# A second home for the last five weight units of every expert, used by odd experts

## The reference

```
combine = einsum("nk,nke->ne", top_w, one_hot(top_idx, N_EXPERTS))   # two experts a token
g = einsum("nd,edf->nef", t, w_gate)                                  # 16 experts, 1024 x 1024 each
u = einsum("nd,edf->nef", t, w_up)
a = silu(g) * u * combine[:, :, None]
y = einsum("nef,efd->nd", a, w_down)                                  # 1024 x 1024 each
x = x + g2 * y ; y_out = rms_norm(x, norm_final)
```

## Time and profile before

| | us |
|---|---|
| median of 3 runs | 836.02 (828.83 to 836.41) |
| the profiled execution, whole | 833.07 |
| its span, first to last instruction | 831.4 |
| TensorE busy / DVE / ACT / POOL | 746.8 / 311.8 / 187.1 / 43.3 |
| experts, first gate matmul to last down matmul | 326.2 to 803.8 |
| mean DMA rate over the span | 314 GB/s |

### The profile page before, as it was taken

One profiled execution on the slowest core, in us unless ns is written; L12 is line 12 of the kernel. 1 busy time (PEld: TensorE's weight loads), 2 busy tenths in 40 slices (PEclk: granted clock), 3 DMA queues, 4 the chain that ended last, 5 costly groups with the idle time before them and its releaser, 6 DMA issues.

```text
span 831.4 us, 22823 instructions
## 1 busy us (share of the span) xinstructions
PE 746.8 (90%) x9748; PEld 412.1 (50%) x9749; DVE 311.8 (38%) x802; ACT 187.1 (22%) x392; POOL 43.3 (5%) x102
## 2 busy tenths in 40 slices
PE   5699986788999988999998999999999999999862
PEld 5345553474644466553552654554544554555232
DVE  3898969997012266211210121211201211121138
ACT  3555340200022133021211122201201112221132
POOL 2000100000010001200000000000000000000000
PEclk9989999957999976999999999999999999999985
DMA  8910369820139992699999999999999999999981
GB/s 340 413 43 2 127 247 410 344 97 7 50 119 334 361 364 95 214 406 410 410 410 411 409 411 411 410 410 411 410 409 379 413 411 410 410 410 410 410 334 76
DMA packets 70027, 261.05 MB, mean 314 GB/s; under 512 B 10540, under 2 KB 10588, under 8 KB 65880
## 3 DMA queue, kind: packets, MB, share of 16 engines
q1 hardware_dynamic: 67832, 257.17, 78.5%
q0 software_dynamic: 1552, 2.99, 0.9%
q10 hardware_dynamic: 592, 0.14, 0.1%
HBM read 252.49 MB, written 9.17 MB: 315 GB/s over the span
## 4 chain that ended last, share of the span: by engine, by line
PE 59%; DVE 10%; DMA 7%; SPq 6%; issue 2%; ACT 1%; DVEq 0%; ACTq 0%
PE ps L1231 23%; PE ps L1238 11%; PE ps L1223 8%; PE ps L1137 7%; DMA ring<-in_moe_w_up 6%; SPq L414 5%; DVE sreg L1592 3%; PE ps L1197 3%; PE ps L1073 3%; DVE scan_t L1584 3%; DMA vreg<-y_scratch 2%; PE ps L1298 1%; SPq L420 1%; PE ps L1081 1%; PE ps L1277 1%
## 5 line engine op out<-in xcount | busy, mean ns | idle before, releaser
L1231 PE MATMUL ps<-ring,vreg 128*32 128x512 f32 x2240 | 245.7, 593 | 13.1 <-DMA ring<-in_moe_w_up 8.2
L1231 PEld LDWEIGHTS ps<-ring,vreg 128*32 128x32 f32 x2240 | 72.3, 110 | 179.4 <-issue 161.2
L1238 PE MATMUL ps<-ring,vreg 128*32 128x256 f32 x2240 | 125.9, 383 | 0.8 <-ACT vreg L816 0.8
L1769 DVE TENSOR_TENSOR vreg<-vreg,ps 128x256 f32<-128x256 f32 x48 | 17.3, 417 | 212.2 <-ACT vreg L811 212.2
L1238 PEld LDWEIGHTS ps<-ring,vreg 128*32 128x32 f32 x2240 | 71.8, 111 | 48.8 <-issue 2.8
L1223 PEld LDWEIGHTS ps<-vreg,sreg 128*128 128x128 f32 x720 | 82.7, 192 | 12.6 <-issue 12.6
L1223 PE MATMUL ps<-vreg,sreg 128*128 128x96 f32 x720 | 86.0, 276 | 0.0
L1787 DVE COPY vreg<-ps 32x256 f32<-32x256 f32 x90 | 38.1, 424 | 99.6 <-PE ps L1238 97.2
L833 ACT ACTIVATE vreg<-ps 32x256 f32<-32x256 f32 x90 | 33.6, 373 | 139.4 <-PE ps L1238 137.6
L1137 PE MATMUL ps<-ring 128*128 128x512 f32 x128 | 58.7, 617 | 1.4 <-issue 0.7
L811 ACT ACTIVATE vreg<-ps 128x256 f32<-128x256 f32 x48 | 15.0, 385 | 196.4 <-PE ps L1231 196.4
(11 more groups left out here) (295 smaller groups left out, 608.0 us busy)
## 6 DMA issues: line engine op xcount, KB each, us to landing
ring<-in_moe_w_down SPq DMA_DIRECT2D x128, 512.0 KB, 12.2
ring<-in_moe_w_gate SPq DMA_DIRECT2D x123, 512.0 KB, 13.2
ring<-in_moe_w_up SPq DMA_DIRECT2D x123, 512.0 KB, 14.4
ring<-in_w_ada SPq DMA_DIRECT2D x24, 1024.0 KB, 11.7
ring<-in_ssm_w_glu SPq DMA_DIRECT2D x8, 1024.0 KB, 13.0
ring<-in_ssm_w_in SPq DMA_DIRECT2D x8, 512.0 KB, 21.7
y_scratch<-sreg SPq DMA_DIRECT2D x6, 512.0 KB, 7.6
sreg<-ada_rows SPq DMA_DIRECT2D x4, 512.0 KB, 8.4
```

Source lines behind the costliest of these rows:

```text
L1231: last = pe.matmul(ps[t][32 * j:32 * j + 32, :], xgT[:, k, 32 * t:32 * t + 32], w[:, :, 256 * j:256 * j + 256], start=(k == 0), stop=(k == ...
L1238: last = pe.matmul(ps[3 + t // 2][32 * dj:32 * dj + 32, 256 * (t % 2):256 * (t % 2) + 256], aT[:, t, c2, 32 * j:32 * j + 32], ring[:, KT + ...
```

## The change

The five buffers are no longer a one-time waiting room: they are a second home for units 7 to 11 of every odd expert. Units 0 to 6 have one place (`SINGLE = 7`), which even and odd experts share; units 7 to 11 have two. TensorE reads each unit where it lies, so the copies by VectorE are gone. For an odd expert the fetches of units 7 to 11 now wait for the expert two before it, or for nothing at the start, and units 0 to 6 as before for the expert just before it. SyncE therefore fetches every expert's units in the order 7, 8, 9, 10, 11, 0, ..., 6. As an instruction names a fixed buffer, the loops of SyncE and TensorE now go over pairs of experts, with the code of an even and of an odd expert in each body. In TensorE's even half the tests whether there is a next expert fall away. What is loaded at the end (`y2c`) and stored (`yo`) moves into the ring, as the old places now hold weights. The total of bytes fetched stays the same. VectorE's, ScalarE's and GpSimd's loops over experts stay.

```diff
@@ -70,6 +70,7 @@
 OOB = 1 << 20
 UNIT = 2048
 NU = 12
+SINGLE = 7
...
@@ -220,12 +221,15 @@
...
-        early_unit = [mod2[:, 0, :, :].rearrange("p r n -> p (r n)"), mod2[:, 1, :, :].rearrange("p r n -> p (r n)"),
-                      h2T[:, :, :].rearrange("p k t -> p (k t)")[:, 0:UNIT],
-                      tmat[:, :, :].rearrange("p g n -> p (g n)"), front[:, :]]
-        yo = ring[:, 8:10, :].rearrange("p a b -> p (a b)")[:, 0:NT * D].rearrange("p (t n) -> p t n", t=NT)
-        y2c = [mod2[:, :, :, :].rearrange("p a r n -> p (a r n)")[:, 0:NT * D].rearrange("p (t n) -> p t n", t=NT),
-               h2T[:, :, :].rearrange("p k t -> p (k t)").rearrange("p (t n) -> p t n", t=NT)]
+        odd_unit = [front[:, :], tmat[:, :, :].rearrange("p g n -> p (g n)"),
+                    mod2[:, 0, :, :].rearrange("p r n -> p (r n)"), mod2[:, 1, :, :].rearrange("p r n -> p (r n)"),
+                    h2T[:, :, :].rearrange("p k t -> p (k t)")[:, 0:UNIT]]
+
+        def unit_of(u, odd):
+            return odd_unit[u - SINGLE] if odd and u >= SINGLE else ring[:, u, :]
+        yo = ring[:, 0:2, :].rearrange("p a b -> p (a b)")[:, 0:NT * D].rearrange("p (t n) -> p t n", t=NT)
+        y2c = [ring[:, 8:11, :].rearrange("p a b -> p (a b)")[:, c * NT * D:(c + 1) * NT * D].rearrange(
+            "p (t n) -> p t n", t=NT) for c in range(2)]
...
@@ -275,7 +279,7 @@
...
-        ld_early = [sem(f"ld_early{u}") for u in range(len(early_unit))]
+        ld_odd = [sem(f"ld_odd{u}") for u in range(SINGLE, NU)]
...
+        def landed(u, odd):
+            return ld_odd[u - SINGLE] if odd and u >= SINGLE else ld_unit[u]
...
@@ -408,45 +415,47 @@
...
-            def load_unit(u, e):
-                if u < KT:
-                    for h, w in enumerate((w_gate, w_up)):
-                        sp.dma_start(ring[:, u, h * D:(h + 1) * D],
-                                     w[0, bass.ds(e, 1), u * P:(u + 1) * P, :].rearrange("a p n -> (a p) n")
-                                     ).then_inc(ld_unit[u], 16)
-                else:
-                    for h in range(2):
+            def load_unit(u, i, odd):
+                def of_pair(w):
+                    return w[0].rearrange("(i two) p n -> two i p n", two=2)[int(odd), bass.ds(i, 1)]
+                for h in ((1, 0) if u == KT else (0, 1)):
+                    if u < KT:
+                        src = of_pair((w_gate, w_up)[h])[:, u * P:(u + 1) * P, :]
+                    else:
                         k = 2 * (u - KT) + h
-                        sp.dma_start(ring[:, u, h * D:(h + 1) * D],
-                                     w_down[0, bass.ds(e, 1), k * P:(k + 1) * P, :].rearrange("a p n -> (a p) n")
-                                     ).then_inc(ld_unit[u], 16)
+                        src = of_pair(w_down)[:, k * P:(k + 1) * P, :]
+                    sp.dma_start(unit_of(u, odd)[:, h * D:(h + 1) * D], src.rearrange("a p n -> (a p) n")
+                                 ).then_inc(landed(u, odd), 16)
...
             for u in (0, 1, 5):
-                load_unit(u, 0)
+                load_unit(u, 0, False)
             for n, u in enumerate((2, 3, 6, 7, 8, 9, 10, 11, 4)):
                 sp.wait_ge(glu_free, min(n + 1, KT))
-                load_unit(u, 0)
-
-            def load_early(u):
-                for h, w in enumerate((w_gate, w_up)):
-                    sp.dma_start(early_unit[u][:, h * D:(h + 1) * D], w[0, 1, u * P:(u + 1) * P, :]
-                                 ).then_inc(ld_early[u], 16)
-            load_early(4)
+                load_unit(u, 0, False)
+
+            load_unit(7, 0, True)
             sp.wait_ge(dve_x1, 6)
-            load_early(3)
+            load_unit(8, 0, True)
             sp.wait_ge(dve_h2, 6)
-            load_early(0)
-            load_early(1)
+            load_unit(9, 0, True)
+            load_unit(10, 0, True)
             sp.wait_ge(pe_logit, NT)
-            load_early(2)
-            for u in range(len(early_unit), NU):
+            load_unit(11, 0, True)
+
+            def load_both(before, i, odd):
+                for u in range(SINGLE, NU):
+                    sp.wait_ge(unit_free, before + (int(odd) * NU + u + 1 - 2 * NU))
+                    load_unit(u, i, odd)
+                for u in range(SINGLE):
+                    sp.wait_ge(unit_free, before + (int(odd) * NU + u + 1 - NU))
+                    load_unit(u, i, odd)
+            for u in range(SINGLE):
                 sp.wait_ge(unit_free, u + 1)
-                load_unit(u, 1)
-            with sp.Fori(2, NE) as e:
-                for u in range(NU):
-                    sp.wait_ge(unit_free, e * NU + (u + 1 - NU))
-                    load_unit(u, e)
+                load_unit(u, 0, True)
+            with sp.Fori(1, NE // 2) as i:
+                for odd in (False, True):
+                    load_both(i * (2 * NU), i, odd)
             sp.wait_ge(y_sent, 16 * (NE - 1))
...
@@ -456,13 +465,12 @@
...
+                sp.wait_ge(dve_pre, NT)
                 with sp.Fori(1, ROUNDS) as r:
-                    with sp.Fori(0, NE) as e:
-                        for u in range(NU):
-                            sp.wait_ge(unit_free, r * (NE * NU) + e * NU + (u + 1 - NU))
-                            load_unit(u, e)
+                    with sp.Fori(0, NE // 2) as i:
+                        for odd in (False, True):
+                            load_both(r * (NE * NU) + i * (2 * NU), i, odd)
                 sp.wait_ge(y_sent, 16 * NE * ROUNDS)
-                sp.wait_ge(dve_pre, NT)
                 load_y2()
...
@@ -1225,47 +1233,56 @@
...
-            def gate_up(k, t):
-                w = ring[:, k, :].rearrange("p (a n) -> p a n", a=2)
+            def gate_up(k, t, odd):
...
-                                     ring[:, KT + j, c2 * D + 256 * dj:c2 * D + 256 * dj + 256],
...
-            def third_gate_up(it):
+            def wait_unit(u, it, two, odd):
+                if u < SINGLE:
+                    pe.wait_ge(ld_unit[u], it * 32 + 32)
+                else:
+                    pe.wait_ge(landed(u, odd), two * 16 + 32)
+
+            def third_gate_up(it, two, odd):
                 for k in range(KT):
-                    pe.wait_ge(ld_unit[k], it * 32 + 32)
-                    gate_up(k, 2)
-
...
-            def expert(it, e, count=None):
...
                     with pe.If(count > 64):
-                        third_gate_up(it)
+                        third_gate_up(it, two, odd)
...
-                with pe.If(e < NE - 1):
+                    wait_unit(k, it, two, odd)
+                    gate_up(k, 0, odd)
+                    gate_up(k, 1, odd).then_inc(unit_free, 1)
+                if odd:
+                    with pe.If(e < NE - 2):
+                        gather_x(it + 1, 0, 5)
+                else:
                     gather_x(it + 1, 0, 5)
...
-                with pe.If(e < NE - 1):
+                if odd:
+                    with pe.If(e < NE - 2):
+                        gather_x(it + 1, 5, KT)
+                else:
                     gather_x(it + 1, 5, KT)
...
-                        pe.wait_ge(ld_unit[KT + kk // 2], it * 32 + 32)
...
@@ -1317,16 +1337,19 @@
...
-            with pe.Fori(0, NE) as e:
+            with pe.Fori(0, NE - 1, 2) as e:
                 n = pe.value_load(counts[0:1, bass.ds(e, 1)], min_val=0, max_val=T)
-                expert(e, e, n)
+                expert(e, e, e, False, n)
+                n = pe.value_load(counts[0:1, bass.ds(e + 1, 1)], min_val=0, max_val=T)
+                expert(e + 1, e, e, True, n)
             v = pe.value_load(cmaxi[0:1, 0:1], min_val=0, max_val=T)
...
@@ -1790,10 +1813,6 @@
...
-            for u in range(len(early_unit)):
-                dve.wait_ge(ld_early[u], 32)
-                dve.wait_ge(unit_free, u + 1)
-                cp(ring[:, u, :], early_unit[u]).then_inc(ld_unit[u], 32)
```

More of the change, by code:

```diff
@@ L1327, in _ @@
                     gather_x(r * NE, 0, KT)
[L1328 to L1329 removed]
+                    with pe.Fori(0, NE - 1, 2) as e:
+                        expert(r * NE + e, r * NE + e, e, False)
+                        expert(r * NE + e + 1, r * NE + e, e, True)
                 pe.wait_ge(y_ev, 12 * NE * ROUNDS + 12)
```

29 lines of the change are left out of this document (15 added, 14 removed).

## The result

The changed kernel takes 900.04 us (median of 4 runs, 898.43 to 900.85), the kernel before 835.65 beside it (4 runs): 1.0795 times as long, 95% interval 1.0743 to 1.0848. That is 64 us slower. I had forecast 863, with 886 as the upper end. The sign and the kind of cause were right; the second rival (all pieces anew) is what happened, at 17 us above the 883 that I gave it.

What follows compares the result with a forecast made beforehand. Weight fetch and TensorE were held close, the fetch bounding with 6 us of TensorE slack. Seven misses, 40.5 us, made TensorE the bound: span 858.3 against 831.4, +26.9 on 836.0 gives 863; own range 856 to 870, 8-in-10 range about 829 to 886.

Steps and rivals of the forecast that it cites:

- the second rival: TensorE's loop: all nine code pieces are fetched anew in each pass, adding 20.3 us for 883; chance 0.22.
- TensorE's code decides: Fetching TensorE's instructions for the longer loop body decides the result; a miss on each of seven branches back costs 40.5 us.
- Nine at once: The changed TensorE loop needs nine 256-instruction pieces, one fetched ahead; no row showed more than five kept.
- I take the miss: At TensorE's branch back one piece is missing each pass, seven times, 40.5 us in all, giving 863; chance 0.46.
- 5.8 us a branch: A TensorE branch back to an unloaded piece costs 5.8 us more than to a loaded one, seven times.
- The second piece, 2.9 us in seven passes: Behind TensorE's branch back, fetching the next piece is only partly hidden: 2.9 us more in seven passes, 20 us.
- Slack of 6 us: TensorE, never starved, would start the last expert 6 us earlier; added cost on TensorE may use that up.
- Earlier restart of the fetch: SyncE waits for expert 0's unit 0, not unit 5, so fetching resumes at 328.0, not 336.80: 8.8 us gained.
- More buffers later on, 1.5 us: Two homes stop the ring filling during long experts, where two slices fell to 372 and 392 GB/s: 1.5 us gained.
- The order gives the gain back; the end is 1.9 us shorter: Last expert: 13.5 us of work behind unit 6 returns all but 0.2 of 10.3 us; tail 1.9 us shorter.
- The case on the faster side: No miss, and the fetch's 10.3 us reach the end with the tail's 1.9: 824; chance 0.06.
- No miss: 834: Rival in TensorE's loop: all nine pieces stay loaded, TensorE ends at 803.6, a shorter tail gives 834; chance 0.26.

Runs made afterwards that it cites:

- e1: Kernel before with only TensorE's expert loop going over pairs, an expert's code twice in its body; 899.24 us, 1.0807.
- e5: Changed kernel with TensorE's loop body written once for both experts of a pair, branching on parity only where buffers differ; 835.6 us, 1.0012.
- f1: Whole changed kernel with 92 instructions, mostly transposes always jumped over, put ahead of TensorE's loop; 829.12 us, 0.9923.
- e9: Changed kernel without even experts' third pass of down, and with 148 instructions of shift, mostly skipped transposes, ahead of TensorE's loop; 830.95 us, 0.999.
- d1: e9 with the last expert's units fetched in the order 0 to 11; 828.59 us, 0.9909.
- f2: f1 with the last expert's units fetched in their order 0 to 11; 826.85 us, 0.9909.
- c1: Whole changed kernel with 124 instructions, mostly transposes always jumped over, put ahead of TensorE's loop; 885.49 us, 1.0599.
- e3: Changed kernel without the even experts' third pass of down in TensorE's main loop; 900.55 us, 1.0808.
- d2: e9 with a skipped stretch of 242 instructions in place of 148 ahead of TensorE's loop; 902.17 us, 1.0783.
- e11: e5 with a pause of already met waits, 23.4 us, ahead of each pair of experts; 1022.87 us.

## Why the prediction was right or wrong, point by point

- **TensorE's code decides.** Right, and shown by e1 (all of the loss), e5 and f1 (none of it).
- **"Nine at once", and five kept at least.** The nine was right, the line now measured: eight pieces stay (e9, d1, f1, f2), nine don't (the other kernels of the table), and the one fetched ahead counts. By that the Trainium skill (page Runtime: NRT & Kernel Launch, section Instruction fetch mechanics), whose 2,048 instructions in blocks of 256 are eight, agrees with the runs; its remark on two lines does not.
- **"I take the miss", one a pass.** This step failed. Nine pieces that follow each other through eight places are all fetched anew, nine packets a pass, as the second rival had it. Its own text had the reason (each throws out the next one needed); I gave it 0.22, for "a fixed place for each piece", of which no row spoke. A body that is too large by one piece loses all of them.
- **5.8 us a branch.** Right: a median of 6.0 us for the seven (one took 7.9), +42.6 where the sum had +40.5. It rested on a single sample.
- **The second piece, 2.9 us in seven passes.** The rival's term that was mis-sized. I had the boundary 58 instructions of gate work behind the jump's target (my own numbers, a start at 8,989 and piece 36 at 9,216, give about 89); it lies at 91, ahead of the target at 137. TensorE had nothing to run meanwhile, and the 20 us became 25.3. The wrong place came from transposes counted as four instructions, which the profile before could have told: the earlier trace rows has 8,761 matmuls and weight loads where I counted 8,944.
- **The clock.** Missing from the sum altogether: 14.3 us. The forecast priced a stall by its length; the 2 to 5 us behind it, run at the lower level, cost 1.4 to 2.7 us more each time. With these terms the sum is 863 + 2.1 + 25.3 + 14.3 = 904.7, 4.7 from the median; in spans it is 858.3 + 41.7 = 900.0 against 898.8, and most of the rest is the 2.9 us that I added for the profiled execution before.
- **Slack of 6 us.** Right: the stalls used it and the last expert's own waits, 11.3 us in all.
- **Earlier restart of the fetch.** Right: the first fetch behind `unit_free` goes out at 327.34 (336.80 before); forecast 328.3.
- **More buffers later on, 1.5 us.** About 1 us of it shows in f1: the two slices that fell to 372 and 392 GB/s before are at 401 and 399 (slices of 385 to 795 us).
- **The order gives the gain back; the end is 1.9 us shorter.** Right where it can be seen, in f1: the last down at 802.74 for 803.6, the tail shorter by 2.2. The case on the faster side named what is still to be had: with the last expert's order put back, TensorE is what ends last (f2, last down at 798.87), at 826.85 us for its 824.
- **No miss: 834.** f1 gave 829.1 beside a kernel before of 835.0: 5.9 us less where I had 2.1. The two traces are 3.3 us apart (spans of 828.1 and 831.4): 1.1 at the last down, before which the experts start 1.4 us earlier (324.82 against 326.24), and 2.2 in the tail. The profiled execution before was itself 2 to 3 us faster than the medians. What is left of the difference, and whether the earlier start is the change's doing, stays open.

## What to carry to other kernels

Before a loop body is unrolled or duplicated, count its instructions on its engine as the trace shows them, and find where its pieces of 256 are cut. Pieces entered and one ahead were free up to eight on TensorE; at nine every pass fetched everything again, which cost 7 to 13 us a pass in these kernels. Code ahead of the loop that is never executed can decide between the two. When a stall on TensorE is priced, add what the matmuls behind it lose at the lower clock, and read the first target of a jump against the next boundary.

## What the runs showed of the hardware that I had not expected

- 32 instructions that are never executed move the time by 56 us (c1 885.49, f1 829.12), since they decide whether the loop lies in seven pieces or eight.
- Where the target of the branch back is no longer held, TensorE goes on 6.0 us after the branch, and at the next piece 5.8 us later (the branch ended at 385.6, the jump's stall at 391.5). This delay, not the bandwidth, is the price: nine fetches are 0.15 MB, under 0.4 us at 410 GB/s. It is 7.0 to 7.1 us where the packet of the piece ahead comes just before the target's (e3, c1, d2).
- TensorE's granted clock was 0.50 for 2 to 5 us behind each of the seven stalls of 6 to 11 us (5 us in the one at 391), and the same behind a pause in which nothing was fetched (e11). In f1's first pass it also fell behind stalls of 1.4 and 2.7 us: 0.64 from 356.0 to 359.5 us.
- A transpose of float32 is one matmul and one weight load; the other float32 matmuls of this kernel are two of each.
